# GpSimd adds one residual piece at four norm boundaries of a three-layer-family transformer on one core

## What is computed

```python
for layer in range(DEPTH):
    mod = (cond @ ada_w[layer] + ada_b[layer])[:, None, :]
    sh1, sc1, g1, sh2, sc2, g2 = jnp.split(mod, 6, axis=-1)
    u = rms_norm(h, norm_g[layer, 0]) * (1.0 + sc1) + sh1
    ...
    h = h + (1.0 + g1) * rms_norm(y, norm_g[layer, 1])
    u = rms_norm(h, norm_g[layer, 2]) * (1.0 + sc2) + sh2
    y = swiglu_ffn(u, ffn_w_in[layer], ffn_w_out[layer])
    h = h + (1.0 + g2) * rms_norm(y, norm_g[layer, 3])
```

## Time and profile before

| | us |
|---|---|
| median of 3 runs | 3188.83 |
| the runs | 3186.51 to 3189.45 |
| the profiled execution's own time | 3186.18 |
| its span in the trace | 3184.2 |
| PE busy / DVE busy / ACT busy / POOL busy | 3128.0 / 1541.0 / 1122.3 / 30.3 |
| mean granted TensorE clock | 0.986 of full speed |

### The profile page before, as it was taken

The page is one execution under the profiler, slowest core; times in us unless marked ns, Lnnn a source line. Parts: engine busy times, 40 slices in busy tenths (PEclk is TensorE's granted clock), DMA queues, the critical chain, the costliest instruction groups (busy, mean ns, idle before and its releaser), DMA issues.

```text
span 3184.2 us, 40595 instructions
## 1 busy us (share of the span) xinstructions
PE 3128.0 (98%) x17534; PEld 2610.1 (82%) x17534; DVE 1541.0 (48%) x2105; ACT 1122.3 (35%) x1643; POOL 30.3 (1%) x44
## 2 busy tenths in 40 slices
PE   8999999999999999999999999999999999999999
PEld 7778988888987777988888767898889867798887
DVE  6667554544255555523334654653334653644242
ACT  5454421224232323422224354432232354433131
POOL 0000000000000000000000000000000000000000
PEclk8999999999999999999998999999999999999999
DMA  7433254542232221223321221222222221122232
GB/s 263 151 113 124 93 176 172 172 138 67 93 93 67 76 71 54 67 93 101 98 99 54 67 73 60 80 85 101 93 95 88 77 67 67 67 93 93 93 106 80
DMA packets 211743, 311.77 MB, mean 98 GB/s; under 512 B 9872, under 2 KB 108272, under 8 KB 211568
## 3 DMA queue, kind: packets, MB, share of 16 engines
q1 hardware_dynamic: 200352, 267.14, 25.3%
q0 software_dynamic: 10880, 41.95, 3.7%
q10 hardware_dynamic: 336, 0.12, 0.0%
HBM read 307.06 MB, written 2.10 MB: 97 GB/s over the span
## 4 chain that ended last, share of the span: by engine, by line
PE 91%; DVE 4%; ACT 3%; DMA 1%; issue 1%; ACTq 0%; SPq 0%; DVEq 0%; POOLq 0%
PE G L1998 62%; PE G L2041 9%; PE G L2002 7%; PE X L2094 1%; DVE yT L1532 1%; PE X L2349 1%; DVE acc L1243 1%; PE G L2020 1%; PE G L2148 1%; PE X L2432 1%; PE X L2191 1%; DVE w_lo L1207 1%; PE X L2439 1%; PE X L2375 1%; PE X L2416 0%
## 5 line engine op out<-in xcount | busy, mean ns | idle before, releaser
L1998 PE MATMUL G<-u_hi,w_hi 128*128 128x512 f32 (+1 forms) x2192 | 883.0, 403 | 3.3 <-issue 3.2
L1998 PE MATMUL G<-u_hi,w_lo 128*128 128x512 f32 (+1 forms) x2192 | 858.7, 392 | 0.0
L1998 PE MATMUL G<-u_lo,w_hi 128*128 128x512 f32 (+1 forms) x2192 | 857.6, 391 | 0.0
L1207 DVE TENSOR_TENSOR w_lo<-raw,w_hi 128x2048 fp32r<-128x2048 f32 (+2 forms) x242 | 544.9, 2253 | 512.2 <-ACT w_hi L624 511.6
L624 ACT CAST w_hi<-raw 128x2048 fp32r<-128x2048 f32 (+2 forms) x242 | 454.7, 1880 | 538.5 <-DMA raw<-in_w_ff 239.4
L1998 PEld LDWEIGHTS G<-u_hi,w_hi 128*128 128x128 f32 (+1 forms) x2192 | 410.1, 187 | 116.8 <-issue 28.9
L1998 PEld LDWEIGHTS G<-u_hi,w_lo 128*128 128x128 f32 (+1 forms) x2192 | 410.2, 187 | 93.7
L1998 PEld LDWEIGHTS G<-u_lo,w_hi 128*128 128x128 f32 (+1 forms) x2192 | 411.2, 188 | 83.8 <-issue 1.7
L1998 PE MATMUL G<-ff_hi,w_hi 128*128 128x512 f32 x448 | 174.9, 390 | 0.0
L1998 PE MATMUL G<-ff_hi,w_lo 128*128 128x512 f32 x448 | 174.4, 389 | 0.0
L1998 PE MATMUL G<-ff_lo,w_hi 128*128 128x512 f32 x448 | 174.3, 389 | 0.0
(11 more groups left out here) (409 smaller groups left out, 4432.5 us busy)
## 6 DMA issues: line engine op xcount, KB each, us to landing
raw<-in_w_ff SPq DMA_DIRECT2D x128, 512.0 KB, 4.4
raw<-in_ffn_w_in SPq DMA_DIRECT2D x88, 512.0 KB, 4.6
ada_raw<-in_ada_w POOLq DMA_DIRECT2D x40, 1024.0 KB, 6.7
raw<-in_w_in SPq DMA_DIRECT2D x64, 512.0 KB, 4.3
raw<-in_attn_w_in SPq DMA_DIRECT2D x96, 256.0 KB, 3.7
raw<-in_ffn_w_out SPq DMA_DIRECT2D x40, 512.0 KB, 4.3
raw<-in_hgrn_w_in SPq DMA_DIRECT2D x32, 512.0 KB, 4.5
raw<-in_attn_w_in SPq DMA_DIRECT2D x24, 512.0 KB, 4.4
```

The lines of the kernel that those rows point to most:

```text
L1207: tt(w_lo[slot][:, 0:nk, 0:w], raw[slot][:, 0:nk, 0:w], w_hi[slot][:, 0:nk, 0:w].bitcast(F32), ALU.subtract).then_inc(s_lo, 1)
L1998: ins = mm(G[0:c1_ - c0, m, :], w[iw][:, k, c0:c1_], xs[ix][:, x0(b) + kk, :], start=first, stop=last, skip_group_check=True)
```

## The change

The add `hT += yT` of tiles 0 to 3, second token half, leaves VectorE's queue at all four boundaries and is put on GpSimd's. Two semaphores link it: `s_scaled` (the multiply by VectorE is done) and `s_pooled` (the add by GpSimd is done), for which ScalarE's square and VectorE's `normed(1, k)` now wait.

```diff
+        s_scaled, s_pooled = sem("second_half_scaled"), sem("second_half_added")
...
                 with pool.Fori(0 if l else ADA_FIRST + 1, ADA_BLOCKS) as b:
                     load(b)
+                for r in range(1, 4) if l else range(1):
+                    pool.wait_ge(s_scaled, r + 1)
+                    nc.gpsimd.tensor_tensor(hT[:, 0:4, half[1]], hT[:, 0:4, half[1]], yT[:, 0:4, half[1]], ALU.add).then_inc(s_pooled, 1)
...
-                        n.take(s_h)
+                        n.take(s_pooled if (hf, i) == (1, 0) else s_h)
...
-                    n.give(tt(yT[:, k, half[hf]], yT[:, k, half[hf]], wide(hf, 4), ALU.mult), s_dve)
+                    n.give(tt(yT[:, k, half[hf]], yT[:, k, half[hf]], wide(hf, 4), ALU.mult), s_scaled if (hf, i) == (1, 0) else s_dve)
 
                 def added(hf, i):
+                    if (hf, i) == (1, 0):
+                        return
...
                     n.own(s_h)
+                    n.take(s_pooled)
```

## The result

The changed kernel takes 3193.52 us (median of 12 runs, 3190.25 to 3197.41). The kernel before, run beside it on the same chip, takes 3185.78 (12 runs, 3182.34 to 3189.45). The ratio is 1.0025, with a 95% interval of 1.0016 to 1.0033, so the change costs 8.0 us (5.1 to 10.5). The profiled execution took 3197.41 us, with a span of 3195.7, and is the slowest of its twelve. It is 11.2 us above the profiled execution of before, and not all of that is the change's.

The account below looks back on a forecast made before the run. TensorE, busy 98% of the span, was taken to bound the kernel. Losses of 2.0 us at the "d" and 3.1 at the "f" boundaries, 5.1 together, on a median of 3188.83 gave 3193.9 us, range 3187.5 to 3200.

Parts of the forecast that it names:

- The add's price: One 128x1024 two-input add on GpSimd: 2.12 us, between bounds of 1.22 and 3.18.
- The "d" boundaries: At hg_out and at_out the square starts 1.01 us later and all of it reaches TensorE: 2.0 us lost.
- hand-over in front: Wake-up and semaphore hand-over before GpSimd's add: 0.15 us allowed.
- nothing was given back: At hg_out and at_out, VectorE's freed time shortens nothing, so the whole 1.01 us each counts.
- The "f" boundaries: At ffn_out01 to at_v and ffn_out11 to z0, step 4 starts 1.48 and 1.60 us later: 3.1 us lost.
- Turns: At at_v and z0, GpSimd's add and VectorE's two-SBUF-input instructions exclude each other; lower(0,3) 1.86 us later.
- Rival 1, side by side: GpSimd's add runs beside VectorE at at_v and z0, gaining 0.64 us there: +1.4 in all, 3190.2; 27%.
- Rival 3, a slow add: At all four boundaries GpSimd's add takes 3.18 us, with turns: +9.3 us, 3198.2; 9%.
- The load: Moved load of ada_w block 12: costed at nothing with 20 us of cover; rival that it is late, 3197, 1%.
- Rival 5: Faster: GpSimd's add at VectorE's rate and beside VectorE, -0.4 us over the four boundaries, 3188.4; 2%.
- Rival 2, the clock: Longer TensorE waits bring new half-clock stretches at two of the four boundaries: 8.1 us in all, 3196.9; 21%.

Follow-up runs that it names:

- e11: The changed kernel run again with no edit, for a second profile: 3195.38 us against 3187.69 for the kernel before, ratio 1.0025.
- e2: The changed kernel with the add on GpSimd only at ffn_out01 and ffn_out11, on VectorE at the other two boundaries: 3189.43 us, ratio 1.0009 to before.
- e3: The kernel before, VectorE keeping its adds, plus a GpSimd add on a spare tile nobody needs then: 3188.34 us, ratio 1.0005.
- e4: The kernel before, VectorE keeping its adds, plus a GpSimd constant fill of a spare tile, and the moved load: 3186.82 us, ratio 1.0001.
- e5: The changed kernel with GpSimd's add cut into four one-tile instructions: 3195.03 us against 3187.02 for the kernel before, ratio 1.0024.
- e1: The changed kernel with the add on GpSimd only at hg_out and at_out, on VectorE elsewhere: 3189.56 us against 3187.05 before, ratio 1.0007.
- e10: The changed kernel with constant matmuls (fillers) ahead of TensorE's boundary waits, about half as many as in a first filled version: 3191.72 us, ratio 1.0011 to before.
- e8: The kernel before with VectorE's add at the "f" boundaries and its square one step later, GpSimd unused: 3185.88 us against 3187.02, ratio 1.0001.
- e9: The kernel before with about half as many constant matmuls ahead of TensorE's boundary waits as e6: 3182.42 us, ratio 0.9984.
- e6: The kernel before with constant matmuls put ahead of TensorE's waits at the four boundaries: 3187.62 us, ratio 0.9998.

## Why the prediction was right, and where its sizes were off

**Time.** 3193.9 was forecast and 3193.52 measured, but the reference point moved: the kernel before ran at 3185.78 there, 3.05 us below the median that I started from. The change itself was forecast at 5.1 us and costs 8.0 (5.1 to 10.5), and 8.0 again in e11. That the two totals agree to 0.4 us is luck: a start 3.05 us too high and a cost 2.6 us too low (5.1 against 7.74 between the medians) cancel. The places and the direction were right, and the prices of the terms that the sum had were off by 0.4 us a boundary at most; it left out the clock.

**The add's price.** 2.12 us forecast, 2.40 and 2.39 measured at "d"; at "f" 2.21 from the split's end. The hand-over in front was 0.08 us (352.09 to 352.17) and not 0.15. The estimate of 2.25 us that the prediction worked out from the Trainium skill (GPSIMD Engine Reference, section "Performance versus the Vector engine") was nearer to all three than my middle of two bounds.

**The "d" boundaries.** Forecast 1.01 us each, 1.21 measured on the chain at hg_out. The 0.20 is the add's 0.28 less 0.07 of hand-over. That nothing was given back held: the waits for the squares are on TensorE, and at hg_out one of 0.5 us became two, of 0.58 and 0.91. The 1.21 is the chain's alone. With the clock's part the boundary lengths grew by 1.69 (hg_out) and 3.98 (at_out).

**The "f" boundaries.** Turns, not side by side. `lower(0,3)` was to end 1.86 us later behind the split and ends 1.70 later (753.03 less 750.54 is 2.49, before 748.31 less 747.52 is 0.79). The boundaries were to grow by 1.48 and 1.60, and grow by 1.11 and 1.32 where the clock is as before (e2). At at_v the rest can be read in the chains, before and then in e2:

```profile
753.39 1.68 PE X L2094 x16
```

```profile
750.42 4.39 PE G L2158 x18
754.82 1.68 PE X L2104 x16
```

From the start of step 3 to the sums behind step 5 TensorE took 5.02 us before (748.37 to 753.39) and 4.40 in e2 (750.42 to 754.82), so 0.62 was given back, where I had counted only the wait of 0.38.

With e3 against e4 the cause is shown and not only argued: an add that reads unrelated data blocks, a write doesn't, and in e5 a shorter read blocks for less. So the engines do not meet only at semaphores, as the first section has it. This is the rule of the Trainium skill, SBUF — State Buffer, section "Who interferes with whom"; the runs agree (`lower` 2.18 us under an add, 0.47 with a fill). Sum of all four: 2 x 1.21 + 1.11 + 1.32 = 4.85 us against 5.1, and e1 and e2 together give 5.3.

**Rival 1, side by side** (27%), is refuted by every held `lower`. **Rival 3, a slow add**, by 2.40. **The load**, by its window: landed at least 22 us ahead of its use (all DMA is idle from 365, the first product comes at 387.92), and by e4, which moves it too and costs nothing. **Rival 5** by both.

**Rival 2, the clock** (21%), came true beside the forecast, and I was wrong to set it against the forecast instead of adding it. It asked for two new stretches at half clock and put the cost at 8.1 us. The first profile has two new ones, at hg_out (363.4 to 366.9) and at z0 (1715.1 to 1718.5), and two that grew (at_out, from 3.4 to 10.2 us, and one in 725 to 733, ahead of at_v's `scaled(1,0)`, where the clock falls from 0.79 to 0.57); e11's has new ones at hg_out and at_v, and the same 10.2 at at_out. Its 8.1 is nearer to the measured 8.0 than the forecast's 5.1. At at_out the cost can be read without the add: 24.82 and 24.83 us with 10.2 us at half clock, 22.19 (e1) and 22.17 (e10) with 3.4. The four boundary lengths grow by 9.6 us in all in the first profile and 10.1 in e11's, where 4.85 are counted without the clock. Over the runs the change loses 4.6 ± 1.1 us more to the clock (47.0 less 42.4). That is the right order for the 3 us between 8.0 and 4.85. Half-clock time that falls in waits counts in the 4.6 and costs nothing, which fits the surplus. I had taken the old stretches at three boundaries as a reason that little could be added; but a stretch can be lengthened: the 6.8 us more at at_out cost 2.6 (24.82 less 22.19), the new 3.4 us at z0 cost 1.5 (27.97 less 26.50 in e2).

**What stays open.** What decides whether a boundary gets a stretch at 1.2 GHz, and how long. Two traces of the changed kernel differ at the same place (at z0, from 1700 on, 17.1 us of half clock in one and 10.2 in the other; TensorE's waits for u_lo there are 4.8 us in the one and 3.7 in the other, and which of the two follows from the other isn't told by a trace). And why the two parts together lose clock time that neither loses alone isn't explained: each part's own count could miss 2 us by its error. The full-clock parts don't add up either: e1 and e2 each have 3.1 us more than before (3146.3 against 3143.2), 6.2 together, the whole change 3.8. With e8, which loses 3.2 us more to the clock and has shorter waits, this says that the split over all runs is no proof of the clock's part; what shows it is the rows at at_out.

## What to carry to other kernels

Before work that reads SBUF moves to GpSimd, look for VectorE instructions that read two SBUF tiles in the time it will run: GpSimd's reading and theirs took turns by whole instructions here (`lower` 2.18 and 2.46 us in place of 0.48), so the idle engine lengthens the busy one. Look also at which queue the result gates: here ScalarE's square stood ahead of the rounding that TensorE needed next. And where TensorE waits for a microsecond or two at a boundary, a few constant matmuls inside the wait can be worth more (5.1 us in e9) than the shifts of Vector work tried here; twice as many (e6) gave it all back.

## What the runs showed that was not expected

- A held instruction shows no wait. `lower` is recorded with 2.46 and 2.18 us and GpSimd's add with 4.32 instead of 0.48 and 2.2 to 2.4; durations have to be compared with those of the same form elsewhere.
- Cutting GpSimd's add in four costs 0.6 us at "d" (3.00 against 2.40) and 0.83 at "f".
- A fill of 128x1024 by GpSimd takes 0.96 us and an add of a tile to itself 1.76, where two different tiles take 2.2 to 2.4.
- Half as many fillers did better than all of them (3182.42 against 3187.62, on two chips; against the kernel before on each, 0.9984 and 0.9998).
- Two executions of the same instructions differ by up to 3 us before the change is reached: the split at 321.8 before starts at 318.7 in e9, and both kernels are the same up to there.
